# One-hot rows moved between engines, a gate loop written out, and a new layout of the gate scratch, in a one-layer hybrid kernel with PEER experts

## The reference

```
idx  = top 16 of 128 x 128 product keys, for each of 8 heads   # 128 experts a token
gate = softmax(best)                                           # 128 weights a token
a    = gelu(einsum('td,tkd->tk', x, u_tab[idx]))               # u_tab: 16384 rows of 1024
y    = einsum('tk,tkd->td', gate * a, v_tab[idx])              # v_tab: 16384 rows of 1024
```

## Time and profile before

| | |
|---|---|
| median of 3 runs | 2303.45 us |
| profiled execution | 2292.26 us, span 2290.5 us |
| TensorE busy | 2173.6 us (95%) |
| VectorE busy | 1438.7 us (63%) |
| POOL busy | 796.5 us (35%) |
| ScalarE busy | 623.6 us (27%) |
| granted clock of TensorE | 0.976 of full speed |
| DMA | 475.54 MB, mean 208 GB/s |

### The profile page before, as it was taken

The page is one execution under the profiler, slowest core; times in us unless marked ns, Lnnn a source line. Parts: engine busy times, 40 slices in busy tenths (PEclk is TensorE's granted clock), DMA queues, the critical chain, the costliest instruction groups (busy, mean ns, idle before and its releaser), DMA issues.

```text
span 2290.5 us, 30680 instructions
## 1 busy us (share of the span) xinstructions
PE 2173.6 (95%) x9868; PEld 1665.6 (73%) x9868; DVE 1438.7 (63%) x3055; ACT 623.6 (27%) x930; POOL 796.5 (35%) x713
## 2 busy tenths in 40 slices
PE   7999998798989999999999898999999999999998
PEld 3554444546987877877777787787888888888886
DVE  4221426334889998878777787324766666666665
ACT  2111012333222223333333233223323222222222
POOL 0000001003225554998989898001222212121220
PEclk7999999898999999999999999999999999999999
DMA  9122124204204444699997899855988888888883
GB/s 338 45 74 72 44 85 181 97 33 160 75 1 153 144 139 138 205 301 309 297 282 250 270 298 288 254 174 210 352 285 294 285 291 289 289 288 290 288 289 146
DMA packets 293477, 475.54 MB, mean 208 GB/s; under 512 B 148871, under 2 KB 150055, under 8 KB 292872
## 3 DMA queue, kind: packets, MB, share of 16 engines
q1 hardware_dynamic: 256520, 340.20, 45.1%
q0 software_dynamic: 36864, 134.23, 16.6%
HBM read 401.76 MB, written 72.61 MB: 207 GB/s over the span
## 4 chain that ended last, share of the span: by engine, by line
PE 78%; POOL 9%; DVE 5%; DMA 3%; issue 2%; SPq 2%; ACT 1%; DVEq 0%; ACTq 0%; POOLq 0%
PE ps L965 30%; PE ps L906 19%; POOL eB L1855 6%; PE ps L624 5%; PE ps L717 3%; PE ps L843 3%; POOL ugat L1824 3%; PE ps L878 3%; PE ps L879 3%; PE ps L683 2%; PE ps L946 2%; SPq L521 2%; PE ps L623 1%; DMA uraw<-in_u_t 1%; PE ps L666 1%
## 5 line engine op out<-in xcount | busy, mean ns | idle before, releaser
L906 PE MATMUL ps<-h2hi,uhi 128*128 128x512 f32 x1024 | 449.8, 439 | 20.3 <-DVE scores L1375 7.7
L906 PE MATMUL ps<-h2hi,ulo 128*128 128x512 f32 x1024 | 404.9, 395 | 0.0
L965 PE MATMUL ps<-vhi,whi 128*128 128x512 f32 x1024 | 399.2, 390 | 5.6 <-DVE wlo L1475 5.6
L906 PE MATMUL ps<-h2lo,uhi 128*128 128x512 f32 x1024 | 403.7, 394 | 0.0
L965 PE MATMUL ps<-vhi,wlo 128*128 128x512 f32 x1024 | 399.1, 390 | 0.0
L965 PE MATMUL ps<-vlo,whi 128*128 128x512 f32 x1024 | 399.0, 390 | 0.0
L1832 POOL DMA_INDIRECT vgat<-in_v_tab,idx x128 | 145.4, 1136 | 660.0 <-DVE y L1485 508.3
L1855 POOL TENSOR_SCALAR eB<-iota,jcur 128x128 f32<-128x128 f32 x384 | 318.1, 841 | 18.8 <-DVE jcur L1440 17.0
L1473 DVE TENSOR_TENSOR vlo<-vraw,vhi 128x1024 fp32r<-128x1024 f32 x128 | 156.8, 1225 | 216.6 <-ACT vhi L1748 216.6
L1748 ACT ACTIVATE vhi<-vraw 128x1024 fp32r<-128x1024 f32 x128 | 135.5, 1061 | 465.8 <-PE ps L965 464.0
L946 PEld LDWEIGHTS ps<-eA,eB 128*128 128x128 f32 x1024 | 192.2, 191 | 93.0 <-POOL eB L1855 25.6
(11 more groups left out here) (270 smaller groups left out, 2993.7 us busy)
## 6 DMA issues: line engine op xcount, KB each, us to landing
uraw<-in_u_t SPq DMA_DIRECT2D x128, 512.0 KB
vraw<-in_v_tab SPq DMA_DIRECT2D x128, 512.0 KB
gelu_scratch<-aout SPq DMA_DIRECT2D x128, 256.0 KB
gate_scratch<-gst SPq DMA_DIRECT2D x16, 2048.0 KB, 14.9
ain<-gelu_scratch SPq DMA_DIRECT2D x128, 256.0 KB, 4.1
gin<-gate_scratch SPq DMA_DIRECT2D x128, 256.0 KB, 4.4
wring<-in_w_ada SPq DMA_DIRECT2D x12, 2048.0 KB, 10.6
wring<-in_w_in SPq DMA_DIRECT2D x6, 2048.0 KB, 8.5
```

What stands on the lines that cost most here:

```text
L906: last = pe.matmul(ps[:, b % 4, :], w[:, b % 2, k, :], h[:, k, LP:T], start=(k == 0 and j == 0), stop=(k == KD - 1 and j == 2))
L965: last = pe.matmul(ps[:, y_bank(t) + h, :], w[:, b, (t - 1) * P:t * P], v[:, b, h * 512:(h + 1) * 512], start=(start and j == 0), stop=(st ...
```

## The change

- eB is made by ScalarE alone, by `slot_keys(m)`: eight activations Abs(j - iota) with the token's column of j as bias, and then one Relu(1 - x) over all eight rows. It is called one block ahead: the first time ahead of `pair(39)`, and then in every block behind the split of u. TensorE waits for it once a block instead of for each row. POOL keeps only its gathers.
- VectorE's step B is written out over the 64 blocks; cur, jcur and their semaphores are gone, eA reads cols_hk itself. ScalarE's rounds are written out too. TensorE's loop stays.
- gate_scratch is laid out as [half of 64 tokens, j, i, token] instead of [i, j, token], so that a store of one part writes 16 KB for each partition in one run instead of 64 runs of 256 B.
- gin has two buffers of four blocks each instead of four of one. One load (`load_gates`) fetches 1 MB for four blocks, in runs of 1 KB, and waits until the group before the last is used. Load 0 stands behind the first four of vraw and ain, load 1 behind the last store of aout (it uses aout's place), the others behind the loads of each fourth block. SP's last loop is written out.

```diff
-    g_dram = nc.dram_tensor("gate_scratch", [NBLK, P, TD], F32, kind="Internal").ap()
+    g_dram = nc.dram_tensor("gate_scratch", [NHALF, P, NBLK, THALF], F32, kind="Internal").ap()
...
-        gin = at("gin", 147, [P, 4, TD])
+        gin = [at(f"gin{b}", k, [P, NHALF, R2, THALF]) for b, k in enumerate((147, 112))]
...
# SP
-                sp_.dma_start(g_dram.rearrange("i p (c t) -> c p i t", t=64)[bass.ds(c, 1)]
-                              .rearrange("o p i t -> (o p) i t")[:, ii], gst[:, half, ii]).then_inc(g_stored[half], 16)
+                sp_.dma_start(g_dram[bass.ds(c, 1)].rearrange("o p i t -> (o p) i t")[:, ii], gst[:, half, ii]
+                              ).then_inc(g_stored[half], 16)
...
+            def load_gates(m):
+
+                if m >= 2:
+                    sp_.wait_ge(w_ready, R2 * (m - 1))
+                sp_.dma_start(gin[m % 2][:].rearrange("p c i t -> p c (i t)"),
+                              g_dram[:, :, R2 * m:R2 * (m + 1), :].rearrange("c p i t -> p c (i t)")).then_inc(g_landed[m % 2], 16)
...
+            load_gates(1)
+            for n in range(R2, NBLK):
+                load_2(n)
+                if n % R2 == R2 - 1 and n + 1 < NBLK:
+                    load_gates((n + 1) // R2)
...
# TensorE
-                        if not dve_row(q):
-                            pe.wait_ge(onehot_j_ready, (it * NB_B + b) * POOL_ROWS + k - k // 4 + 1)
+                        if k == 0:
+                            pe.wait_ge(onehot_j_ready, it * NB_B + b + 1)
...
# VectorE
-            def step_b(it, first):
-                if not first:
-                    dve.wait_ge(onehot_j_ready, it * POOL_ROWS * NB_B)
-                    dve.wait_ge(onehot_ready, it * P)
-                dd = bass.ds(it * P, P)
-                dve.tensor_copy(jcur[:], cols_hk[:, 1, dd]).then_inc(jcur_ready, 1)
-                dve.tensor_copy(cur[:], cols_hk[:, :, dd]).then_inc(cur_ready, 1)
-                dve.wait_ge(cur_ready, it + 1)
...
-                        if dve_row(q):
-                            dve.tensor_scalar(eB[:, b % 2, k], iota[:], cur[:, 1, q:q + 1], None, ALU.is_equal)
...
-            loop(dve, NTD, step_b)
+            for n in range(BLK_A, BLK_C):
+                m = n - BLK_A
+                for k in range(TB):
+                    q = TB * m + k
+                    if q >= RING:
+                        dve.wait_ge(onehot_used, q + 1 - RING)
+                    dve.tensor_scalar(eA[:, q % RING], iota[:], cols_hk[:, 0, q:q + 1], cols_hk[:, 2, q:q + 1],
+                                      ALU.is_equal, ALU.mult).then_inc(onehot_ready, 1)
+                    if k == 4:
+                        split_u(n + 1, n + 1)
...
# ScalarE
+            def slot_keys(m):
+
+                act.wait_ge(cl_drained, m // NB_B + 1)
+                if m >= 2:
+                    act.wait_ge(onehot_used, TB * (m - 1))
+                for k in range(TB):
+                    q = TB * m + k
+                    last = act.activation(eB[:, m % 2, k], iota[:], ACT.Abs, bias=cols_hk[:, 1, q:q + 1], scale=-1.0)
+                seq(last)
+                act.activation(eB[:, m % 2], eB[:, m % 2], ACT.Relu, bias=1.0, scale=-1.0).then_inc(onehot_j_ready, 1)
...
+                if n == BLK_A - 1:
+                    slot_keys(0)
                 pair(n, n % 4, False, False)
...
                     split_u(n + 1, b + 1, False)
                     if b == 0 and not first:
                         slot_gelu(it - 1, second)
+                    if n + 1 < BLK_C:
+                        slot_keys(n + 1 - BLK_A)
                     stage(it, b, first)
                     gelu(n, b, False)
...
# POOL
-                if b == 0:
-                    pool.wait_ge(jcur_ready, it + 1)
-                if n >= 2:
-                    pool.wait_ge(onehot_used, TB * (n - 1))
-                for k in range(TB):
-                    if not dve_row(TB * b + k):
-                        pool.tensor_scalar(eB[:, b % 2, k], iota[:], jcur[:, TB * b + k:TB * b + k + 1], None, ALU.is_equal
-                                           ).then_inc(onehot_j_ready, 1)
```

More of the change, by code:

```diff
@@ L425, in bass_hybrid_layer @@
         a_landed = [sem(f"a_landed{b}") for b in range(4)]
-        g_landed = [sem(f"g_landed{b}") for b in range(4)]
+        g_landed = [sem(f"g_landed{b}") for b in range(2)]
         vhi_ready = sem("vhi_ready")
@@ L564, in _, with load_2 @@
             store_g(NTD * 2 - 1, 1, 1)
[L567 to L579 removed]
+            def load_2(n):
+                b = n % R2
+                if n >= R2:
+                    sp_.wait_ge(vhi_ready, n - R2 + 1)
+                    sp_.wait_ge(vlo_ready, n - R2 + 1)
+                sp_.dma_start(vraw[:, b], v_tab[n * P:(n + 1) * P, :]).then_inc(v_landed[b], 16)
+                if n >= R2:
+                    sp_.wait_ge(whi_ready, n - R2 + 1)
+                    sp_.wait_ge(wlo_ready, n - R2 + 1)
+                sp_.dma_start(ain[:, b], a_dram[n]).then_inc(a_landed[b], 16)
+            def load_gates(m):
[3 more added lines that the diff above has]
+                              g_dram[:, :, R2 * m:R2 * (m + 1), :].rearrange("c p i t -> p c (i t)")).then_inc(g_landed[m % 2], 16)
             for n in range(BLK_C, NBLK):
@@ L591, in _ @@
                         sp_.wait_ge(a_stored[b], 16 * (BLK_C // 4))
-                        load_2(b, b, True)
+                    for b in range(R2):
+                        load_2(b)
+                    load_gates(0)
             for b in range(4):
                 sp_.wait_ge(a_stored[b], 16 * (NBLK // 4))
-            with sp_.Fori(1, NBLK // 4) as it:
-                for b in range(4):
-                    load_2(it * 4 + b, b, False)
+            load_gates(1)
[3 more added lines that the diff above has]
+                    load_gates((n + 1) // R2)
             sp_.wait_ge(h_full, NBLK)
@@ L1417, in split_u, with dot @@
                 dve.tensor_tensor(ulo[:, b % 2], uraw[:, b % 4], uhi[:, b % 2].bitcast(F32), ALU.subtract).then_inc(ulo_ready, 1)
[L1419 to L1426, removed]
+            def dot(g):
+                r, k = g // DOTS_IT, g % DOTS_IT
+                if k == 0 and r:
+                    dve.wait_ge(dots_gelu, r)
+                if g:
+                    dve.wait_ge(dot_done, g)
+                dve.wait_ge(u_gathered[g % GSLOT], 16 * (g // GSLOT + 1))
+                dve.tensor_tensor_reduce(junk[:], ugat[:, g % GSLOT], h2row[:], 1.0, 0.0, ALU.mult, ALU.add,
@@ L1461, in _ @@
-            loop(dve, NTD, step_b)
+            for n in range(BLK_A, BLK_C):
[8 more added lines that the diff above has]
+                        split_u(n + 1, n + 1)
+                if m % NB_B == 2 and m >= NB_B:
+                    slot_weights(m // NB_B - 1)
+                for e in range(DOTS_B):
+                    dot(DOTS_B * m + e)
@@ L1496, in _ @@
             slot_weights(NTD - 1)
-            weight(0, 0, 16)
+            weight(0, 0)
             step_2(0, True, False)
@@ L1734, in step_b @@
                         slot_gelu(it - 1, second)
+                    if n + 1 < BLK_C:
+                        slot_keys(n + 1 - BLK_A)
                     stage(it, b, first)
                     gelu(n, b, False)
-            step_b(0, True, False)
-            step_b(1, False, True)
-            with act.Fori(2, NTD) as it:
-                step_b(it, False, False)
+            for it in range(NTD):
+                step_b(it, it == 0, it == 1)
             def high_v(n, s, pos, first):
```

44 lines of the change are left out of this document (12 added, 32 removed).

## The result

The median of four runs is **2243.3 us** (2242.7 to 2244.6) against 2297.6 (2289.6 to 2304.2) of the kernel before: a ratio of **0.977, 95% interval 0.975 to 0.980**. The profiled execution took 2244.6 us, its span 2242.8, 47.7 less than before. Forecast: 2247, with 2246.5 for that execution.

What follows compares the result with a forecast made beforehand. TensorE bounds the second half; step B had 53.1 us of excess from late table loads, loop ends and POOL's pace. Terms -19.4 - 4.8 - 25.6 + 4 = -45.8 from 2292.3 gave 2246.5, stated as 2247 us, range 2234 to 2276.

Steps and rivals of the forecast that it cites:

- eB off POOL: Step B's 64 blocks: moving eB rows to ScalarE removes all but 3 of 22.4 us, -19.4 (bounds -12 and -22.4).
- VectorE written out: VectorE's back edges in step B: half of 9.8 us goes, TensorE's loop may keep the rest; -4.8 (0 to -9.8).
- gate stores, B and C: Blocks 40 to 127: merged stores stop SP standing and uraw arriving late, -25.6 of 26.6 us (bounds -20 and -26.6).
- gate loads: Second half: 1 MB loads in 1 KB pieces arrive in time, costing 0, up to +4 us.
- entry: Block 40: ScalarE's first eB rows delay the split and POOL's ulo, TensorE idles; +4 us (bounds +2 and +6).
- rival 3: ScalarE in step B: Abs or Relu forces table reloads each block, 68 us more, 2315; chance 0.06.
- Rival 1: Step B: ScalarE becomes the pace at 7.7 us a block, 25 us more, 2272; chance 0.12.
- Rival 2: SP's queue: uraw stays late behind the 2 MB stores, so that gain is lost, 2273; chance 0.10.
- three late uraw: Step B: slow gate stores delay uraw table loads in three of 64 blocks, 20.9 us of excess.
- POOL's pace: Step B: POOL's eB rows and gathers take 7.45 us a block, slowing some 30 blocks; 22.4 us of excess.
- Rival 4: Step B: little to see, block runs at 7.7 us and half the late loads stay, 2285; chance 0.06.
- a wait for gin: Second half: TensorE waiting for gate data in gin was named as a sign the prediction is wrong; no size given.

Runs made afterwards that it cites:

- e7: Changed kernel with block 40 split ahead of ScalarE's first eB rows and the second gate load issued early, behind the first: 2245.2 us, 0.979 of the kernel before.
- e9: Changed kernel with eight more Abs a block on ScalarE, into a spare tile nobody reads: 2299.0 us, 1.003 of the kernel before.
- e4: Changed kernel with TensorE's step B written out as well instead of looped: 2242.3 us, 0.978 of the kernel before.
- e1: Kernel before the change with only the new gate layout (16 KB stores, 1 MB gate loads): 2283.1 us, 0.997 of the kernel before.
- e6: Changed kernel with the second gate buffer at another address, its load issued behind the first: 2242.2 us, 0.977 of the kernel before.
- e2: Changed kernel with the old gate layout (256 B stores, one 256 KB gate load a block): 2309.8 us, 1.009 of the kernel before.
- e3: Changed kernel with VectorE's step B back in a loop of 16 blocks with its copies: 2253.5 us, 0.982 of the kernel before.

## Why the prediction was right, step by step

The sum was right. Of its five terms three came out within 3 us (eB, gate stores, entry) and two were mis-sized by 5 us or more (loop ends, gate loads), and the gains in step B are no separate terms at all.

| step | predicted | gone or come in after |
|---|---|---|
| eB off POOL | -19.4 | -22.4, all of that excess is gone |
| VectorE written out | -4.8 | -9.8, all of it |
| gate stores, B and C | -25.6 | -20.9 and -6.2 |
| gate loads | 0 (up to +4) | +5.5 in this execution, +1.0 to +7.6 in the others with these loads |
| entry | +4 | +4.45 (block 40: excess 0.48 before, 4.93 after) |

The last column sums to -49.4. With +2.8 at the front, -1.7 in block 39 and 0.5 of block 40 that stands in two rows it is the 47.7, but for 0.1. Block 39 is shorter because of the entry's new order. VectorE multiplies the weights there (L1402, 128x128), and the multiply that fell beside POOL's ulo of block 40 took 1.91 us (912.03 before). In after that ulo comes later and the multiply takes 0.29. In e7 the ulo is early again: the multiply takes 1.92 and block 39 10.1 us, as before. So the entry's net price is 2.8, not 4.45.

- **eB to ScalarE: right, and its price too.** 5.8 us a block were forecast, the rows give about 5.9. An Abs was 396 ns long where I took 367, and its starts stood 0.29 apart where I took 0.26. No table load stands in the 64 blocks, and gelu's line (L1682) still has two in all: rival 3 is refuted, and here the trace agrees with the page's Table sets (the Trainium skill, "ScalarE: Activation LUTs"). Rival 1 is refuted by the period of 7.33, and e9 shows where its bound lies.
- **Half of the loop ends stay: wrong.** "TensorE keeps its own loop of 16 blocks" and I left it half of the cost. It has none (e4), and no block of 9 to 12 us stands at its edges. By the Trainium skill ("Runtime: NRT & Kernel Launch", Instruction fetch mechanics) a taken branch out of the fetched window stalls. VectorE's 2.12 us in "issue" agree with that, TensorE's edges do not show it; whether TensorE's loop leaves its window, no run tells.
- **Gate stores: right in the change, wrong as a separate term.** Rival 2, that uraw stays late, is refuted: in step B no issue of SP lasts over 1.4 us and uhi never waits for uraw, in e1 as in after. But alone the layout took 12.1 us off step B, not 20.9, and the rows with the written-out loop added 11.4 where 19.4 + 4.8 - 4 = 20.2 should have gone. I had read "three late uraw" and "POOL's pace" off one trace as if each would vanish by itself. They hid each other, and the layout also made the gathers later. The two smaller waits for uraw (blocks 60 and 68) I had counted as POOL's pace, and its "some 30 blocks" are 25. The gate store of 2 MB still slows what flies beside it, also in 16 KB pieces; it is harmless because POOL, now free, issues its gathers 13.2 us ahead (issue at 982.34, dot product at 995.50 after) and not 7.7. Of the Trainium skill's rule that pieces want at least 512 B for full rate ("DMA: Bandwidth & Descriptors", Specifications) the rows show the direction: 14.9 us to landing before, 11.7 in e1.
- **Gate loads at nothing: wrong in size.** The second load goes out at 1528.18 just ahead of the ain of block 4 (1529.29), which lands so late that its product starts at 1546.11. TensorE idles 2.90 us and then runs matmuls of 0.63 instead of 0.39, the 1.2 GHz level (granted clock 0.84 from 1549 to 1560 us). That is outside the term's own bound of +4, and the sign that I had named, a wait for gin, was a wait for ain. That the gate load ahead of it is the cause is borne out by e6 and e7, where the wait at block 4 is gone. My cover, "TensorE stands three blocks behind the loads", did not hold at the first reload.
- **Rival 4**, little to see, needed a pace of 7.7 us and half of the late loads; neither is there.

The errors of the first two terms, -3.0 and -5.0, and of the gate stores, -1.5, were made good by the gate loads (+5.5) and by the front (+2.8), which is chance. That the median lies 3.7 us from the forecast is no sign that the split was known that well.

## What to carry to other kernels

Two causes of delay read off one trace are not two gains: ask of each what the other is hiding, and whether a faster stage makes the next transfer due sooner. Removing POOL's rows and the loop ends alone made this kernel slower, fixing the stores alone did next to nothing, and both together gave 2.3%. For a prefetch, compare its lead (issue to first use) with its landing time beside the largest transfer in flight, not with the median.

## What was not expected of the hardware

- A gather landed in 5.2 us, beside a 2 MB store of 16 KB pieces in 10.8 (e1), and the issuing queue did not stand. Behind 8192 pieces of 256 B it stood 8.0 and 13.7 us at a time in the issue of a small store, and the gathers there landed in 7.2 to 8.0 (e2). Behind the first gate load, 1 MB in pieces of 1 KB, it stood 3.2 us (at 1428.16 in after).
- A multiply of 128x128 on VectorE that takes 0.29 us took 1.9 to 2.1 when it started beside POOL's subtraction of 128x1024 (2.38 us), and ended 0.15 us behind it (four cases: two before, one in after, one in e7). The reductions and reciprocals beside the same subtraction kept their length.
- Rows of 128x128 on VectorE that last 0.28 and 0.34 us start 0.20 and 0.25 us apart. Lengths added up overstate a back-to-back group by 38%.
- A loop's back edge stood 2.12 us on VectorE (e3) and cost TensorE nothing (e4, 0.01 us over two edges).
